# Expert gathers bounded by an index, expert rows stored by a bounded scatter of GpSimd

## What is computed

```python
def hier_moe(h, w_group, b_group, w_router, b_router, w_gate, w_up, w_down):
    x = h.reshape(bsz * t, D_MODEL)                       # 576 x 1024
    g_sel = argmax(x @ w_group + b_group)                 # 1 of 4 groups
    top_v, top_i = top_k(e_logits[g_sel], 2)              # 2 of its 8 experts
    top_w = softmax(top_v) * p_g
    hg = einsum('nd,edf->nef', x, w_gate)                 # 32 experts, hidden 256
    hu = einsum('nd,edf->nef', x, w_up)
    act = silu(hg) * hu * gates                           # gates: 0 but for the two picked
    return einsum('nef,efd->nd', act, w_down)
```

## Time and profile before

| | us |
|---|---|
| median of 3 runs | 1954.74 |
| lowest and highest | 1953.57, 1957.83 |
| the profiled execution | 1952.98 |
| its span, first to last instruction | 1951.4 |
| PE busy | 1381.1 (71%) |
| DVE busy | 402.0 (21%) |
| ACT busy | 233.6 (12%) |
| POOL busy | 169.5 (9%) |

### The profile page before, as it was taken

One profiled execution on the slowest core, in us unless ns is written; L12 is line 12 of the kernel. 1 busy time (PEld: TensorE's weight loads), 2 busy tenths in 40 slices (PEclk: granted clock), 3 DMA queues, 4 the chain that ended last, 5 costly groups with the idle time before them and its releaser, 6 DMA issues.

```text
span 1951.4 us, 16081 instructions
## 1 busy us (share of the span) xinstructions
PE 1381.1 (71%) x6073; PEld 706.0 (36%) x6073; DVE 402.0 (21%) x785; ACT 233.6 (12%) x517; POOL 169.5 (9%) x208
## 2 busy tenths in 40 slices
PE   2999965888775767757179999376619657766750
PEld 1555432556335322222045443255414442222210
DVE  1000044543023101101300000441430231110104
ACT  1000003632010000000100000230010100000001
POOL 0200002311000100000200000120130000000002
PEclk9999987998985878878579999695559658887875
DMA  4313025588720699997332200002216118999954
GB/s 144 108 43 140 0 95 168 155 318 319 316 77 4 240 420 390 396 394 291 120 131 65 76 0 0 11 33 52 38 63 288 52 33 351 401 402 398 370 201 154
DMA packets 108068, 354.13 MB, mean 181 GB/s; under 512 B 25786, under 2 KB 41146, under 8 KB 83282
## 3 DMA queue, kind: packets, MB, share of 16 engines
q1 hardware_dynamic: 90514, 292.97, 39.8%
q0 software_dynamic: 12864, 43.26, 6.4%
q10 hardware_dynamic: 4608, 16.78, 2.1%
HBM read 316.95 MB, written 36.02 MB: 181 GB/s over the span
## 4 chain that ended last, share of the span: by engine, by line
PE 56%; DMA 21%; DVE 9%; SPq 3%; ACT 3%; issue 3%; POOL 2%; PEldq 1%; POOLq 1%; DVEq 0%; ACTq 0%; PEld 0%
DMA moe_wgu<-in_moe_w_up 14%; PE ps L1191 8%; PE ps L441 7%; PE ps L1440 7%; PE ps L294 6%; PE ps L1429 4%; PE ps L452 4%; PE ps L1207 3%; PE ps L246 2%; DMA fox_arena<-in_cache_k 2%; PE ps L1012 2%; PE ps L1753 1%; ACT rows L214 1%; SPq L967 1%; DMA moe_wgu<-expert_rows,moe_slot 1%
## 5 line engine op out<-in xcount | busy, mean ns | idle before, releaser
L1191 PE MATMUL ps<-moe_wgu,moe_xT 128*64 128x512 f32 x1024 | 262.1, 671 | 145.8 <-DMA moe_wgu<-in_moe_w_up 140.6
L1191 PEld LDWEIGHTS ps<-moe_wgu,moe_xT 128*64 128x64 f32 x1024 | 80.1, 155 | 306.0 <-issue 160.0
L441 PE MATMUL ps<-turned,fox_arena 128*128 128x512 f32 (+1 forms) x512 | 141.4, 440 | 11.6 <-DMA fox_arena<-in_fox_w_in 11.6
L1440 PE MATMUL ps<-mwblk,turned 128*128 128x512 f32 (+1 forms) x320 | 138.8, 594 | 0.9 <-DVE mkT L1489 0.9
L1207 PE MATMUL ps<-moe_wd,moe_aT 128*64 128x512 f32 x512 | 116.8, 598 | 2.3 <-ACT moe_y L1266 2.3
L246 PE MATMUL ps<-cst,rows 128*128 128x128 f32 (+1 forms) x160 | 46.9, 425 | 85.4 <-DVE rows L227 85.4
L441 PEld LDWEIGHTS ps<-turned,fox_arena 128*128 128x128 f32 x512 | 78.7, 194 | 74.4 <-issue 62.6
L1302 DVE TENSOR_TENSOR moe_hid<-moe_sg,ps 128x256 f32<-128x256 f32 x32 | 13.5, 421 | 408.0 <-ACT moe_sg L1256 408.0
L1440 PEld LDWEIGHTS ps<-mwblk,turned 128*128 128x128 f32 (+1 forms) x320 | 56.7, 179 | 82.1 <-issue 81.1
L1429 PE MATMUL ps<-turned,mwblk 128*128 128x512 f32 (+1 forms) x256 | 71.9, 445 | 12.5 <-DMA mwblk<-in_mlstm_w_in 12.5
L1170 POOL DMA_INDIRECT moe_xg<-h_rows,moe_src_row x32 | 30.2, 945 | 546.9 <-PE ps L1183 419.8
(11 more groups left out here) (277 smaller groups left out, 1502.5 us busy)
## 6 DMA issues: line engine op xcount, KB each, us to landing
moe_wgu<-in_moe_w_gate SPq DMA_DIRECT2D x64, 1024.0 KB, 17.3
moe_wgu<-in_moe_w_up SPq DMA_DIRECT2D x64, 1024.0 KB, 19.3
moe_wd<-in_moe_w_down SPq DMA_DIRECT2D x64, 1024.0 KB, 13.8
fox_arena<-in_cache_k SPq DMA_DIRECT2D x32, 512.0 KB, 7.7
fox_arena<-in_cache_v POOLq DMA_DIRECT2D x32, 512.0 KB, 9.4
expert_rows<-moe_y ACTq DMA_DIRECT2D x32, 512.0 KB, 8.2
fox_arena<-in_fox_w_in SPq DMA_DIRECT2D x6, 2048.0 KB, 8.8
mwblk<-in_mlstm_w_in SPq DMA_DIRECT2D x6, 2048.0 KB, 9.5
```

The costliest lines, as they stand in the source:

```text
L441: mm = pe.matmul(ps2[:, g % 4, a:b], wblk[:, blk % 3, c, cc * P:(cc + 1) * P], turned[:, c, a:b], start=(c == 0), stop=(c == KC - 1))
L1191: mm = pe.matmul(ps[h, 2 + p % 2, :].rearrange("s (k f) -> s k f", k=2), xT[:, c, h], wgu[:, s, half, :, c, :], start=(c == 0), stop=(c == ...
L1440: mm = pe.matmul(ps[0:r, k % 8, :], turned[:, c, n * P:n * P + r], wblk[:, blk % 3, c, :], start=(c == 0), stop=(c == KC - 1))
```

## The change

1. `token` holds the token's number less 65536 (`NOWHERE`); DVE adds 65536 to what PE gives. A used slot has its token again, an unused one has 65536. Each gather is given a bound, the last token's number; a row whose index is beyond it is skipped.
2. DVE computes a second list of indices, `dst_row`: the slot's own row in `y_dram` (the new constant `own_row`), plus 65536 where the slot is unused. In the place of one copy it has four operations.
3. The rows of `y` are stored by POOL, by an indirect DMA with `dst_row` and a bound. ACT issues no DMA any more and doesn't wait for both halves; POOL does (`scatter`).
4. POOL's order is: gathers of pairs 0 and 1; then for p = 0 to 15 the gather of p+2, the scatter of p-1; then the last scatter, the wait for all stores, `used` and the branches.
5. `xg` is set to zero by POOL at the phase's start, ahead of the first gather.
6. `fill_rows` writes all 3200 rows of `y_dram` in the place of the last 1152, in seven DMAs in the place of three.
7. `y_out` and `more_out` are lasting semaphores; `cleaned` is new.

```diff
--- before.py
+++ after.py
@@ -42,12 +42,13 @@
 ROUND = 1.5 * 2.0 ** 23
 EPS = 1e-6
 NEG = -1e30
+NOWHERE = 2.0 ** 16
 
 
 CONSTS = [("ident", P), ("neg_causal", P), ("neg_causal_t", P), ("before", P), ("ones", PAST + SS),
           ("dec_mask", SB * SAMP), ("samp_mask_t", SAMP), ("same", SB),
           ("selpair", MPAIRS * P), ("iota_slot", SLOT), ("iota_tile", TILES),
-          ("rev4", GROUPS), ("rev32", EXP), ("token", NT), ("valid", NT), ("minus_half", MH * NT)]
+          ("rev4", GROUPS), ("rev32", EXP), ("token", NT), ("own_row", TILES // 2), ("valid", NT), ("minus_half", MH * NT)]
 OFFSET, CW = {}, 0
 for _name, _w in CONSTS:
     OFFSET[_name] = (CW, _w)
@@ -87,7 +88,8 @@
     c["rev32"][:] = EXP - np.arange(EXP)
     tok = np.arange(NT)[None, :] * P + i
     c["valid"][:] = tok < TOK
-    c["token"][:] = np.where(tok < TOK, tok, 0)
+    c["token"][:] = np.where(tok < TOK, tok - NOWHERE, 0)
+    c["own_row"][:] = np.arange(TILES // 2)[None, :] * P + i
     c["minus_half"][:] = -0.5
     return np.concatenate([c[n] for n, _ in CONSTS], 1)
 
@@ -195,7 +197,7 @@
 
         def fill_rows(sp):
 
-            left = (TILES - EXP) * SLOT
+            left = TILES * SLOT
             while left:
                 n = min(left // P, NT - 1)
                 row = TILES * SLOT - left
@@ -399,7 +401,7 @@
                         sp.wait_ge(q_done if blk < 5 else k_done, 8 if blk == 4 else 4)
                     sp.dma_start(wblk[:, blk % 3], w_view[:, :, blk * 512:blk * 512 + 512]).then_inc(w_in[blk % 3], 16)
                 fill_rows(sp)
-                sp.wait_ge(filled, 48)
+                sp.wait_ge(filled, 16 * -(-TILES * SLOT // PROMPT))
                 sp.wait_ge(v_kept, 2 * NT)
                 for dst, src in ((("v_prompt", "v_sample"), v), (("k_prompt", "k_sample"), knat)):
                     if src is knat:
@@ -991,6 +993,9 @@
             rowsel = sb(tag + "rowsel", [P, 2 * NT, SLOT], where=mx)
             tilesel = sb(tag + "tilesel", [P, 2 * NT, TILES], where=mx)
             src_row = sb(tag + "src_row", [P, TILES // 2], U32, where=mx)
+            dst_row = sb(tag + "dst_row", [P, TILES // 2], U32, where=mx)
+            source = sb(tag + "source", [P, TILES // 2], where=mx)
+            empty = sb(tag + "empty", [P, TILES // 2], where=mx)
             et = sb(tag + "et", [1, MORE, EXP], where=mx)
             ef = sb(tag + "ef", [1, MORE + 1], where=mx)
             ctl = sb(tag + "ctl", [1, MORE + 1], I32, where=mx)
@@ -1121,7 +1126,10 @@
                 ch(dve.tensor_scalar(ef[:, 0:MORE], ef[:, 0:MORE], float(EXP - 1), None, ALU.min))
                 ch(dve.tensor_copy(ctl[:], ef[:]))
                 dve.wait_ge(src_done, 1)
-                ch(dve.tensor_copy(src_row[:], ps[:, 2, 0:TILES // 2]))
+                ch(dve.tensor_scalar(source[:], ps[:, 2, 0:TILES // 2], NOWHERE, None, ALU.add))
+                ch.step(dve.tensor_copy(src_row[:], source[:]))
+                ch(dve.tensor_scalar(empty[:], source[:], NOWHERE, NOWHERE, ALU.is_ge, ALU.mult))
+                ch(dve.tensor_tensor(dst_row[:], empty[:], const("own_row"), ALU.add))
 
             phases.append(dict(sp=sp_, pe=pe_, act=act_, dve=dve_))
 
@@ -1135,12 +1143,13 @@
             y = sb(tag + "y", [P, 2, D], where=mx)
             BASE = layer * (STATIC // 2)
             x_in = [lasting(tag + f"x_in{u}") for u in range(2)]
-            y_out = [sem(tag + f"y_out{u}") for u in range(2)]
+            y_out = [lasting(tag + f"y_out{u}") for u in range(2)]
+            cleaned = sem(tag + "cleaned")
             xt_done, xt_kept, gu_done, silu_done = sem(tag + "xt_done"), sem(tag + "xt_kept"), sem(tag + "gu_done"), sem(tag + "silu")
             a_ready, at_done, at_kept, y_done = sem(tag + "a_ready"), sem(tag + "at_done"), sem(tag + "at_kept"), sem(tag + "y_done")
             y_kept_a, y_kept_v = sem(tag + "y_kept_a"), sem(tag + "y_kept_v")
             more_w, more_x = sem(tag + "more_w"), lasting(tag + "more_x")
-            more_out = sem(tag + "more_out")
+            more_out = lasting(tag + "more_out")
 
             def used(eng):
                 return eng.value_load(ctl[0:1, MORE:MORE + 1], min_val=0, max_val=MORE)
@@ -1163,19 +1172,39 @@
                             sp.dma_start(wd[:, 0, half], i["moe_w_down"][layer, bass.ds(e, 1)].rearrange("a (p c) n -> p (a c) n", c=2)
                                          ).then_inc(more_w, 16)
 
+            def gather(pool, p, s, landed):
+
+                pool.indirect_dma_start(xg[:, s, :], None, h_dram[layer], bass.IndirectOffsetOnAxis(ap=src_row[:, p:p + 1], axis=0),
+                                        bounds_check=TOK - 1, oob_is_err=False).then_inc(landed, 16)
+
+            def scatter(pool, p, s, landed):
+
+                pool.wait_ge(y_kept_a, p + 1)
+                pool.wait_ge(y_kept_v, p + 1)
+                pool.indirect_dma_start(y_dram, bass.IndirectOffsetOnAxis(ap=dst_row[:, p:p + 1], axis=0), y[:, s, :], None,
+                                        bounds_check=TILES * SLOT - 1, oob_is_err=False).then_inc(landed, 16)
+
             def pool2(pool):
+                pool.memset(xg[:], 0.0).then_inc(cleaned, 1)
+                pool.wait_ge(cleaned, 1)
+                for p in range(2):
+                    gather(pool, p, p, x_in[p])
                 for p in range(STATIC):
-                    if p >= 2:
-                        pool.wait_ge(xt_done, p - 1)
-                    pool.indirect_dma_start(xg[:, p % 2, :], None, h_dram[layer],
-                                            bass.IndirectOffsetOnAxis(ap=src_row[:, p:p + 1], axis=0)).then_inc(x_in[p % 2], 16)
+                    if p + 2 < STATIC:
+                        pool.wait_ge(xt_done, p + 1)
+                        gather(pool, p + 2, p % 2, x_in[p % 2])
+                    if p:
+                        scatter(pool, p - 1, (p - 1) % 2, y_out[(p - 1) % 2])
+                scatter(pool, STATIC - 1, (STATIC - 1) % 2, y_out[(STATIC - 1) % 2])
+                for s in range(2):
+                    pool.wait_ge(y_out[s], 16 * (STATIC // 2))
                 live = used(pool)
                 for q in range(MORE // 2):
                     with pool.If(live > 2 * q):
                         pool.wait_ge(xt_done, STATIC + q)
-                        pool.indirect_dma_start(xg[:, 0, :], None, h_dram[layer],
-                                                bass.IndirectOffsetOnAxis(ap=src_row[:, STATIC + q:STATIC + q + 1], axis=0)
-                                                ).then_inc(more_x, 16)
+                        gather(pool, STATIC + q, 0, more_x)
+                        scatter(pool, STATIC + q, 0, more_out)
+                        pool.wait_ge(more_out, 16 * q + 16)
 
             def turn_rows(pe, p, s):
 
@@ -1264,8 +1293,6 @@
 
                 act.wait_ge(y_done, p + 1)
                 act.activation(y[:, s, 0:512], ps[:, 5, :], ACT.Copy).then_inc(y_kept_a, 1)
-                act.wait_ge(y_kept_a, p + 1)
-                act.wait_ge(y_kept_v, p + 1)
 
             def act2(act):
                 for p in range(STATIC + 1):
@@ -1277,18 +1304,16 @@
                         if p >= 3:
                             act.wait_ge(y_out[s], 16 * ((p - 1) // 2))
                         keep_rows_act(act, p - 1, s)
-                        act.dma_start(y_dram[(p - 1) * P:p * P, :], y[:, s, :]).then_inc(y_out[s], 16)
-                for s in range(2):
-                    act.wait_ge(y_out[s], 16 * (STATIC // 2))
                 live = used(act)
                 for q in range(MORE // 2):
                     p = STATIC + q
                     with act.If(live > 2 * q):
                         silu_gate(act, p)
                         keep_hidden(act, p)
+                        act.wait_ge(y_out[0], 16 * (STATIC // 2))
+                        if q:
+                            act.wait_ge(more_out, 16 * q)
                         keep_rows_act(act, p, 0)
-                        act.dma_start(y_dram[p * P:(p + 1) * P, :], y[:, 0, :]).then_inc(more_out, 16)
-                        act.wait_ge(more_out, 16 * q + 16)
 
             def keep_turned(dve, p):
 
```

## The result

The changed kernel takes 1924.36 us (median of 4 runs, 1921.91 to 1932.8) against 1954.15 for the kernel before (median of 4). The profiled execution took 1921.91 us (span 1920.3), 31.1 less than that of before.

What follows compares the result with a forecast made beforehand. The prediction took the expert phases to be bound by a loop through the landing of gate and up weights. Fixed costs of +6.0 us and -2.9 from row transfers gave +3.1 on 1954.74: 1957.9 us, range 1942 to 1970.

Steps and rivals of the forecast that it cites:

- The loop through the landing of gate and up: Expert phases: a 37.0 us period of two steps, 14.4 us TensorE plus 22.6 us until step A's weights land.
- the 22.6 us: Issue to landing of A's weights: six weight blocks 15.5 us, three row transfers 3.9, start after an empty queue 3.2.
- a short and a long step: Steps A and B of a period, with one wait for weights, before A; the pattern was taken as unchanged.
- 2.84 for 3: Row transfers counted in the loop after the change, at 1.3 us each: -0.2 us a period, -2.9 over 14.
- B's pair: Step B's scatter and gather: scatter expected at 795.5 to 799.6, some 15% of the gather before the landing at 800.8.
- the factor 0.9: Each gather and scatter: the fullest DMA engine keeps 7.2 of 8 rows, so a transfer takes 0.9 of its time.
- The dry place: Stretch where the weight queue is nearly empty, 776 to 779.5; gather A there was said to cost the loop nothing.
- rival 1: Left-out rows spread evenly over the engines: -1.2 us a period, -17 in all, total 1944 us; chance 0.30.
- rivals 2 and 3: Rival 2: nothing saved where it counts, 1961 us, chance 0.17. Rival 3: gathers lose the dry place, 1972, chance 0.13.
- The fixed terms: Per layer: clearing +2.0, index operations +0.5, phase end +0.6, fewer semaphores -0.1; sum 3.0, +6.0 us for both.
- The end: End of an expert phase: GpSimd's last scatter and branches finish after TensorE's, +0.6 us a layer.
- The fill: Filling 3200 rows in place of 1152: ends near 195, under TensorE's projection, and costs nothing.

Runs made afterwards that it cites:

- e13: Kernel before, with SyncE issuing gate and up weights of a pair ahead of down's weights of the previous pair: 1909.05 us, ratio 0.9763.
- e12: e8 with e13's order of the weight loads and nothing else changed: 1883.49 us, ratio 0.9625 to the kernel before.
- e8: e3 with the clearing of xg by GpSimd moved into the routing phase: 1919.57 us, ratio 0.9788 to the kernel before.
- e1: Changed kernel with NOWHERE set to 0, so no row is skipped and all are moved: 1944.79 us, ratio 0.9937 to the kernel before.
- e3: Changed kernel with each expert's used slots dealt evenly over the runs of four partitions: 1924.74 us, ratio 0.9844 to the kernel before.
- e4: Changed kernel with used slots packed, filling one pair of four-partition runs after the other: 1941.28 us, ratio 0.9919 to the kernel before.
- e9: Changed kernel unaltered, measured again: 1931.27 us, ratio 0.9872 to the kernel before.
- e10: Kernel before, with SyncE storing y behind the gate and up weights in its own queue, nothing skipped: 1922.65 us, ratio 0.9832.
- e5: Kernel before, with each gather from pair 4 on held back until both copies of y are done: 1959.64 us, ratio 1.0014.
- e2: Changed kernel with the gather issued earlier, ahead of the same step's scatter, still skipping: 1934.38 us, ratio 0.9869 to the kernel before.
- e6: e1 with e2's early gather, so GpSimd stores every row and gathers keep their old place: 1968.76 us, ratio 1.0054 to the kernel before.
- e11: e10 with bounded gathers and xg cleared in the routing phase: 1924.91 us, ratio 0.982 to the kernel before.
- e7: Kernel before, with bounded gathers and the clearing, ACT still storing all rows: 1951.32 us, ratio 0.9966.

## Why the prediction was wrong

**What bounds the kernel: right.** The loop through the landing of gate and up, of 14.4 us of TensorE and 22.6 of transfers, is there before and after, e13, which breaks it, is the fastest of the kernels that leave nothing out, and e12 gains 32 us over e8 by the ratios (36 by the medians) by breaking it.

**The step that failed: what the new places of the transfers do to the 22.6 us.** The prediction kept the pattern of a short and a long step and asked only how much of three row transfers still falls into the long one: 2.84 for 3, -0.2 us a period. Measured was -2.4. In the change and in e1 a step has one pair, scatter and gather on one queue, and B's pair comes too late for the loop: the packets of the scatter issued at 790.08 start at 794, just before the landing at 795.5. So the loop holds one pair, not three transfers. For e1 that gives 14.4 + 15.5 + 2 x 1.3 + 3.2 = 35.7, and 35.7 was measured; for e3, at 0.62 of each, 34.7, and 34.65 was measured; for e4, at 1.0, 35.7, and 35.5. This sum was made after the runs and holds for those three. For the change it gives 35.5 at the factor 0.9 (21.1 us from issue to landing, and the period shown above has 21.2), but the mean of its periods was 34.5, and 34.8 in e9. The factor may be too high: which engine is fullest changes from pair to pair, and the one that keeps most over a whole phase keeps 0.82 and 0.85 by the same count of the routing. That takes off 0.2 us. The 0.5 to 0.8 us left I can't place, and so the agreement with e3 may be chance.

**The dry place was the loss, not a shelter.** The prediction read the earlier trace rows as a place where a gather costs nothing and asked whether the change would lose it. But around it the engines moved 309 GB/s, and that shortage, 2 us a period, was just what could be won without leaving a byte out: e10 and e13 win it, and end at 34.8 and 34.7 us. Nothing in the sum priced the possibility that a shift of the transfers would close it. The change doesn't win it: its new places alone close 1.2 us of it (e1), but with the rows left out the place is dry again. So the 2.4 us of the period are 1.2 of new places and 1.2 of skipped rows, and with the rows dealt another 1.6 us lie open behind the loop, which e12 takes. The earlier trace rows hides the shortage: it adds up to 98.2% of the time of the engines, but its 2.59 us for a block are stretched. At e10's 421 GB/s a block takes 2.49.

**Why moving both shortens the period, and moving one doesn't: argued, not shown.** Rows in GpSimd's queue alone get every second packet, those in two queues every third each. e1, 750 to 753, then e5, 751 to 754:

```profile
q1 hardware_dynamic: 114, 0.81, 64.1%
q0 software_dynamic: 114, 0.41, 34.0%
```

```profile
q1 hardware_dynamic: 91, 0.61, 48.6%
q0 software_dynamic: 95, 0.39, 31.5%
q10 hardware_dynamic: 85, 0.29, 23.8%
```

The counts are equal within ten packets. The Trainium skill ("DMA: Bandwidth & Descriptors", Queues, rings and completion order) says that each engine goes round its queues packet by packet; these equal counts agree. In e5 both transfers are over sooner and hold the weights back harder while they last; in e1 they stay longer (q0 has packets from 748 to 756 and from 768 to 776, eight microseconds of each step), and the steps come out even. That the pattern tips for that reason no run has isolated.

**The skipping.** The factor was right in kind: the fullest engine decides (e4), so rival 1, rows spread evenly, is refuted, though its 1944 lay nearest; rivals 2 and 3 are, since the period neither stayed nor grew. The 7.2 rows of 8 are the count for layer 0; for layer 1 the same count gives 7.6. And skipping was worth more than forecast, 0.9 to 1.2 us a period between e1 and the change (0.2 was the whole forecast).

**The fixed terms** were near. Chain before the first gather of layer 0, and VectorE ahead of it:

```profile
634.30 1.81 POOL moe_xg L1188
636.17 0.56 issue
636.76 0.20 issue
636.96 4.17 DMA moe_xg<-h_rows,moe_src_row
```

```profile
632.79 0.19 DVE L1129 TENSOR_SCALAR moe_source<-ps 128x25 f32<-128x25 f32 x1 [0.44 <-PE ps L1032]
633.01 0.18 DVE L1130 CAST moe_src_row<-moe_source 128x25 uint32<-128x25 f32 x1
633.10 0.17 DVE L1131 TENSOR_SCALAR moe_empty<-moe_source 128x25 f32<-128x25 f32 x1
633.30 0.19 DVE L1132 TENSOR_TENSOR moe_dst_row<-moe_empty,cst 128x25 uint32<-128x25 f32 x1
```

The clearing costs 1.86 (2.66 from its start to the gather, where 0.80 stood; 2.0 forecast), the four operations the 0.5 forecast. The end was wrong in its order: TensorE's branches still come last, and GpSimd's drain behind them grew instead.

```profile
919.72 3.01 PEldq L1269
923.05 0.03 PEldq L1928
923.10 2.67 POOLq L1926
```

+0.6 for the branches was 0, while the drain takes 2.67 us and took 1.36 before. Together 3.7 a layer where 3.0 was forecast. The drain's 1.3 lie behind the end of the phase as counted here (the phase after it takes 26.4 us and took 25.3). The other 2.4 don't show in the phases' total, since the steps outside the twelve periods shortened too (their rest is 159.5 us and was 160.1).

**The fill** was free, as forecast:

```profile
154.12 26.45 SPq L204 DMA_DIRECT2D expert_rows<-x  x7
...
259.09 0.39 SPq L409 DMA_DIRECT2D out_v_prompt<-fox_arena  x1
```

The last of seven is issued by 180.6, none took over 23.7 us to land, no packet of it runs after 194 (195 was forecast), and v goes out at 259.09, where it went at 259.05.

**What the experiments' expectations missed.** e1 came out between its two theories, neither back at 1950 to 1958 nor within 5 us of the change. e3 was to go on to 1905 to 1915, as if each term moved the period by its own size, and e4 to lose 4 to 8 us (more only if an engine's lag adds up) and lost 17. e2 was to be up to 10 us faster than the change or 4 to 8 slower, and was the same within its interval. e5 was to gain by itself and didn't; e6 cost 11 us by its ratio, where 2 to 8 were expected. e11 was to save 3 to 8 us over e10 and saved none. e13 and e12 did better than expected (46 us below before and not 20 to 28; 1883 and not 1898 to 1908), though their periods are near the forecast: no expectation counted the earlier weights at the phase's start.

## What to carry to other kernels

In a loop bound by transfers, work out first what the bytes of a period need at the rate of a full queue; here 34.9 us against a period of 37.0. The difference is what reordering can win, and closing it comes before leaving bytes out, since those count fully only when nothing makes the queue run dry again (e12 against e13: 26 us; e11 against e10, where only the gathers skip: none). Look again after the change: a shorter period with the same bytes a second, as here, means that the queue still runs dry, or that the bytes left out are uneven over the engines. When a change moves transfers between queues and places, don't keep the pattern of the steps fixed in the sum: price the case in which it evens out.

## What the runs showed of the hardware

- A row skipped by the bound still leaves a packet, of a few bytes. Packets under 512 B grew by 3649 from before to the changed kernel and by 65 only to e1; 3584 rows are skipped. On the change's queue the gather and the scatter have 144 packets as ever.
- An indirect transfer with a bound takes GpSimd 0.99 (gathers of e7) to 1.02 us (gathers of the changed kernel) to issue, medians, 0.94 without.
- GpSimd's drain at the end of an expert phase takes 2.67 us in the kernels in which it scatters (the change, e1, e6) and 1.36 in those in which it doesn't (before, e7, e10). Scattering isn't the only thing that makes it long: before has the same 2.67 us at 306.3 and 495.5, at the ends of phases without a scatter.
- The scatter of the changed kernel lands 3.2 us after its issue at best and its gather 3.4 us, sooner than the 4.4 of before. That is the rows left out and not the bound: with all rows moved, e1's gather needs 4.3 at best. Lines L1184 and L1177:

```profile
DMA to landing us min/median/max: 3.2/9.1/10.2
...
DMA to landing us min/median/max: 3.4/11.1/12.6
```
